# Storing the rotated queries and keys of a dilated attention branch stream by stream

## The reference

```python
def dilated_window_attention(q, k, v, window, dilation):
    B, S, H, dh = q.shape
    L = S // dilation
    def to_sub(t):
        return t.reshape(B, L, dilation, H, dh).transpose(0, 2, 1, 3, 4).reshape(B * dilation, L, H, dh)
    o, lse = banded_attention(to_sub(q), to_sub(k), to_sub(v), window // dilation)
    ...
outs, lses = [], []
for g, (window, dilation) in enumerate(DIL_GROUPS):
    q_g, k_g, v_g = (heads(t, DIL_HEADS, HEAD_DIM) for t in parts[3 + 3 * g: 6 + 3 * g])
    o_g, lse_g = dilated_window_attention(rope(q_g, pos), rope(k_g, pos), v_g, window, dilation)
```

## Time and profile before

| | |
|---|---|
| median of 3 runs | 5552.71 us |
| profiled execution, device time | 5561.61 us |
| its span on the slowest core (core 5) | 5560.1 us |
| its cores | 5526.5 to 5560.1 us |
| TensorE (PE) busy on that core | 5365.4 us, 96% |
| DVE busy | 2707.3 us, 49% |
| ACT busy | 2872.0 us, 52% |
| mean granted TensorE clock | 0.990 of full speed |

### The profile page before, as it was taken

One profiled execution on the slowest core, in us unless ns is written; L12 is line 12 of the kernel. 1 busy time (PEld: TensorE's weight loads), 2 busy tenths in 40 slices (PEclk: granted clock), 3 DMA queues, 4 the chain that ended last, 5 costly groups with the idle time before them and its releaser, 6 DMA issues.

```text
span 5560.1 us, 82537 instructions; the slowest of 8 cores (5526.5 to 5560.1 us)
## 1 busy us (share of the span) xinstructions
PE 5365.4 (96%) x30664; PEld 2677.9 (48%) x30664; DVE 2707.3 (49%) x4106; ACT 2872.0 (52%) x4224; POOL 568.5 (10%) x1281
## 2 busy tenths in 40 slices
PE   6899989999999999999999999999999999999999
PEld 3454534444455544444555554444455555344444
DVE  5466544433456655443345665543245566444232
ACT  5787742224876763232577765332277776432121
POOL 2011110000011111010001111101000011000000
PEclk9999999999999999999999999999999999999999
DMA  7655467666224456767422536666732253764442
GB/s 154 92 91 102 78 209 233 214 218 171 72 78 127 127 169 216 230 221 233 125 75 83 147 102 211 233 219 197 233 100 75 85 151 105 252 218 160 160 159 102
DMA packets 353408, 866.04 MB, mean 156 GB/s; under 512 B 163712, under 2 KB 184192, under 8 KB 303872
## 3 DMA queue, kind: packets, MB, share of 16 engines
q1 hardware_dynamic: 341504, 788.15, 44.2%
q0 software_dynamic: 11520, 72.62, 8.9%
HBM read 789.61 MB, written 163.58 MB: 171 GB/s over the span
## 4 chain that ended last, share of the span: by engine, by line
PE 87%; ACT 5%; DMA 4%; DVE 2%; issue 1%; POOL 1%; SPq 0%; POOLq 0%; ACTq 0%; DVEq 0%
PE ps L581 86%; ACT arena L597 4%; DVE arena L608 2%; PE ps L590 1%; DMA arena<-wallbf 1%; DMA oall<-arena 1%; DMA arena<-arena 1%; DMA arena<-x 1%; ACT arena L601 0%; POOL arena L645 0%; SPq L622 0%; DVE arena L616 0%; DMA arena<-cf 0%; POOL arena L643 0%; DVE arena L604 0%
## 5 line engine op out<-in xcount | busy, mean ns | idle before, releaser
L581 PE MATMUL ps<-arena 128*128 128x512 bf16 (+3 forms) x29576 | 5317.5, 341 | 148.6 <-ACT arena L597 71.6
L581 PEld LDWEIGHTS ps<-arena 128*128 128x128 bf16 x29576 | 2612.4, 101 | 2799.9 <-issue 426.7
L597 ACT ACTIVATE arena<-ps 128x512 f32<-128x512 f32 (+6 forms) x2384 | 1725.3, 759 | 1765.8 <-PE ps L581 1675.8
L608 DVE TENSOR_TENSOR arena<-arena 128x1024 bf16<-128x1024 bf16 (+7 forms) x1133 | 761.2, 674 | 404.2 <-ACT arena L597 373.3
L597 ACT ACTIVATE arena<-arena 128x1024 bf16<-128x1024 f32 (+4 forms) x904 | 805.5, 910 | 137.9 <-PE ps L590 66.1
L608 DVE TENSOR_TENSOR arena<-arena,ps 128x512 bf16<-128x512 f32 (+1 forms) x480 | 379.8, 791 | 894.3 <-PE ps L581 893.1
L608 DVE TENSOR_TENSOR arena<-ps,arena 128x512 bf16<-128x512 f32 (+2 forms) x872 | 657.2, 769 | 279.2 <-PE ps L581 146.8
L597 ACT ACTIVATE arena<-ps,arena 128x512 f32<-128x512 f32 x384 | 263.7, 687 | 634.4 <-PE ps L581 633.9
L616 DVE SCALAR_TENSOR_TENSOR arena<-arena,ps 128x512 f32<-128x512 f32 x384 | 263.6, 687 | 450.7 <-PE ps L581 243.6
L604 DVE CAST arena<-ps 128x256 bf16<-128x256 f32 (+1 forms) x410 | 210.9, 516 | 264.3 <-PE ps L581 258.7
L616 DVE SCALAR_TENSOR_TENSOR arena<-ps,arena 128x1024 f32<-128x1024 f32 (+1 forms) x128 | 138.5, 1082 | 298.7 <-POOL arena L645 298.0
(11 more groups left out here) (16 smaller groups left out, 335.1 us busy)
## 6 DMA issues: line engine op xcount, KB each, us to landing
arena<-wallbf SPq DMA_DIRECT2D x209, 1024.0 KB, 6.0
arena<-wallbf SPq DMA_DIRECT2D x128, 1088.0 KB, 6.4
arena<-x SPq DMA_DIRECT2D x128, 512.0 KB, 6.7
out<-arena SPq DMA_DIRECT2D x128, 512.0 KB, 4.1
arena<-cf SPq DMA_DIRECT2D x192, 256.0 KB, 3.5
arena<-ftall SPq DMA_DIRECT2D x96, 384.0 KB, 3.8
ftall<-arena SPq DMA_DIRECT2D x264, 128.0 KB, 5.7
arena<-out SPq DMA_DIRECT2D x64, 512.0 KB, 5.1
```

Of the source, the lines that this page charges most:

```text
L581: return e.matmul(out(), lhsT=lhsT, rhs=rhs, start=start, stop=stop, skip_group_check=True)
L597: return R.add([("act", cact(n), [lambda e: e.activation(out=lz(out), in_=lz(in_), func=func, **kw)])], r=r, w=w, fence=fence)
L608: return (eng, c, [lambda e: e.tensor_tensor(out=lz(out), in0=lz(in0), in1=lz(in1), op=op)])
```

## The change

Queries and keys of a round are stored by stream: token i*d+r goes to place r*(2048/d)+i of its row. The adds of the rotation write to these places, in the order i, then r, so that successive elements of an instruction land 2048/d elements apart (1024 bytes with dilation 4, 256 bytes with dilation 16), while they read `T2` and `T1` in order as before. The score matmuls pick their 128 keys and 2 x 128 queries by `pos`, that is, 128 neighbouring elements. With dilation 1 both orders are the same. The values, `tok` for them, and `ND` stay as they are.

```diff
+                    def streams(v, dil=dil, tc=tc):
+                        n = 512 // dil
+                        return v.rearrange("p (r i) -> p i r", r=dil)[:, tc * n:(tc + 1) * n, :]
+
                     for which in range(2):
...
                         if which == 0:
                             for e in range(2):
                                 pr = slice(64 * e, 64 * e + 64)
-                                R.add([a_tt("dve", QZ[pr, e, tsl], lambda T=T2, pr=pr: ps(T)[pr, :], T1[pr, :], ALU.add, 512)],
-                                      r=[T2, T1[pr, :]], w=[QZ[pr, e, tsl]])
+                                o = streams(QZ[pr, e, :])
+                                R.add([a_tt("dve", o, lambda T=T2, pr=pr: ps(T)[pr, :].rearrange("p (i r) -> p i r", r=dil),
+                                            T1[pr, :].rearrange("p (i r) -> p i r", r=dil), ALU.add, 512)], r=[T2, T1[pr, :]], w=[o])
                         else:
-                            R.add([a_tt("dve", KT[:, tsl], lambda T=T2: ps(T), T1, ALU.add, 512)], r=[T2, T1], w=[KT[:, tsl]])
+                            o = streams(KT)
+                            R.add([a_tt("dve", o, lambda T=T2: ps(T).rearrange("p (i r) -> p i r", r=dil),
+                                        T1.rearrange("p (i r) -> p i r", r=dil), ALU.add, 512)], r=[T2, T1], w=[o])
+
+                def pos(r_, b_):
+                    return slice((r_ * nb + b_) * 128, (r_ * nb + b_ + 1) * 128)
...
-                        qz = QZ[:, :, tok(r_, qb)]
+                        qz = QZ[:, :, pos(r_, qb)]
                         mms = []
-                        rd = [qz, KT[:, tok(r_, qb)]]
+                        rd = [qz, KT[:, pos(r_, qb)]]
                         if hp_:
-                            mms.append(((lambda T=S_: ps(T, 256)), KT[:, tok(r_, qb - 1)], qz, True, True))
-                            rd.append(KT[:, tok(r_, qb - 1)])
-                        mms.append(((lambda T=S_: ps(T, 256, 256)), KT[:, tok(r_, qb)], qz, True, True))
+                            mms.append(((lambda T=S_: ps(T, 256)), KT[:, pos(r_, qb - 1)], qz, True, True))
+                            rd.append(KT[:, pos(r_, qb - 1)])
+                        mms.append(((lambda T=S_: ps(T, 256, 256)), KT[:, pos(r_, qb)], qz, True, True))
```

## The result

The changed kernel is slower: ratio 1.0434 to the kernel before, 95% interval [1.0324, 1.0543], about 241 us (180 to 302). The forecast was 0.9% faster. Its profiled execution took 5779.22 us (before: 5561.61), on its slowest core a span of 5777.7 us. The ratios here leave out executions in which the cores of one die ran longer at a lower clock, and the medians on record contain some of those.

A forecast was written before the change was run, and what follows sets the result against it. PE was taken to bound the stage: 62 us gained on score matmuls minus 11 us of DVE delay gives 51 us, so 5502 us, 0.9% faster; range 5482 to 5532 (chance 0.76).

The forecast's parts named there:

- the pace forecast: Score matmuls with dilation 4 and 16 run at dilation 1's 0.11 us each, group mean near 273 ns.
- 62 of 66.8 us: Score matmuls: 66.8 us off PE's list, of which 62 us reach the end by PE's share of the chain.
- I take +0.39 us: Each of 192 scattered DVE adds gets +0.39 us, priced by the stepped fp32 add into ND; 75 us of DVE time.
- The bounds I gave: Extra time of a scattered add: from nothing up to +2.1 us, PE's own factor of 4 for a step of 16.
- The sign of failure that the prediction named: If the new adds stand at 1.5 us or more, or the instruction order differs, the prediction fails there.
- +0.39 fits: Projection parts: DVE has 0.55 to 0.90 us free an add, so the added +0.39 us has room.
- the 11 us of delay: PE's waits for DVE behind the new adds lengthen: 6.2 us in the first sequence, 4.7 in the other three.
- Rival (b): Projection parts: adds cost +2.1 us by PE's step-of-16 factor, DVE limits, loss 203 us, time 5756; chance 0.04.
- The scheduler gets the same costs.: Scheduler counts columns and elements, not steps, so order changes only if a dependency does; nothing counted for it.

The follow-up runs named there:

- the reads alone: Kernel before, with score matmuls reading 128 neighbouring elements while the adds still write in token order; ratio 0.9941 [0.992, 0.9962], 33 us faster.
- the price list: Kernel before plus 16 kinds of DVE adds, each issued 4 times; in order 0.68 us, scattered fp32 1.03 us, scattered bf16 2.42 us.

## Why the prediction was wrong

**The bound and the gain.** PE bounds this stage, and the score matmuls got the pace forecast: 248.2 us busy instead of 318.7, with 273 ns in all rounds. What was off is the share that reaches the end. I took 62 of 66.8 us from PE's share of the chain, and let PE's other waits stay as they were; the reads alone gave 33 [21, 44]. In the profiles PE's idle time grew by 19 us, 10 of it waits for DVE. The rest of the 29 us missing is not explained.

**The step that failed: "I take +0.39 us".** The new add costs +1.75 us. The reason given was the same engine, operation and number of elements; the row differed in the width of the element written, and the price list shows that this is what decides. The bounds I gave, nothing to +2.1 us, held the value; I chose near the wrong end, and gave the other end 0.04. The sign of failure that the prediction named, adds of 1.5 us or more, is what the trace shows.

**"+0.39 fits" and the 11 us of delay.** The argument itself stood: at +0.36 us the change stays a gain, and the difference to the reads alone is 6 us, inside the intervals.

**Rival (b)** is what happened, with its mechanism and place: DVE sets the pace of the projection parts. That its +2.1 us an add came near +1.75 is luck, for it was PE's factor for a step of 16. Its size of the loss was short. At +1.75 it gives (1.75 - 0.72) x 192 - 62 = 136 us (2 us less with 0.73, the mean of the earlier trace rows); measured 241, or 218 between the two profiles. 29 us of the difference is the smaller gain of the reads; another part is likely the clock, since the matmuls of 512 columns alone were busy 54 us longer.

**"The scheduler gets the same costs."** I used this to say that the order stays, which it did, and counted nothing. That was the second step that failed; the slow adds cost as much as they did only together with it: an order made for adds of 0.69 us leaves PE waiting where the other order has matmuls for it. Told the price, the kernel with the same adds is 20 us slower than the kernel before instead of 241; with the 33 us that the reads gain, the adds then cost about 53 us, an estimate from these two ratios.

## What to carry to other kernels

Price a scattered write by a row with the same element width; if there is none, keep the whole range and say that the sign of the forecast hangs on it. Reorder where the step falls on a read of PSUM, which was free here, and keep writes in runs. Where an order is fixed from costs before the launch, give it the new cost of every instruction that the change makes slower, before judging the change.

## What was not expected of the hardware

A DVE add of 512 elements a partition took 0.68 us in order. Written as bf16 it took 0.72 us with a step of 4 bytes, 1.29 with 8 bytes and 2.42 with hops of 256 or 1024 bytes, while fp32 with hops of 512 or 2048 bytes took 1.03. Reading PSUM with a step of 4 or 16 fp32 elements left it at 0.68 us, the same as in order.
